# Last block: the first two up-projection tiles on rows without the second row factor, and two feature blocks to an operation

## The reference, cut to what matters

```python
        mix_out = merged @ w_out[l]
        h_res = h_res + rmsnorm_2(mix_out, g_mix_post[l])

        h2 = rmsnorm_2(h_res, g_ffn_pre[l])
        up = centred_dwconv(h2 @ w_up[l], conv_w_ffn[l], conv_b_ffn[l])
        a, v = jnp.split(up, 2, axis=-1)
        ffn_out = (jax.nn.gelu(a) * v) @ w_down[l]
        h_res = h_res + rmsnorm_2(ffn_out, g_ffn_post[l])
```

## Time and profile before

| | |
|---|---|
| median of 3 runs | 1059.67 us (1059.06 to 1060.96) |
| the profiled execution | 1059.63 us |
| its span | 1057.5 us |
| mean granted TensorE clock | 0.986 |
| TensorE matmul busy | 1004.1 us, 95% of the span |
| DVE, ACT, POOL busy | 581.2, 521.3, 521.7 us |
| chain that ended last | PE 71%, DVE 15%, ACT 10%, issue 3%, DMA 1% |

### The profile page before, as it was taken

The page is one execution under the profiler, slowest core; times in us unless marked ns, Lnnn a source line. Parts: engine busy times, 40 slices in busy tenths (PEclk is TensorE's granted clock), DMA queues, the critical chain, the costliest instruction groups (busy, mean ns, idle before and its releaser), DMA issues.

```text
span 1057.5 us, 15122 instructions
## 1 busy us (share of the span) xinstructions
PE 1004.1 (95%) x6334; PEld 897.3 (85%) x6334; DVE 581.2 (55%) x798; ACT 521.3 (49%) x684; POOL 521.7 (49%) x160
## 2 busy tenths in 40 slices
PE   7979999999999998999999999999998799888897
PEld 6867789999888887789998887999898699888775
DVE  4688875888422544546886223262254567777732
ACT  6445446554333566545654334544444554455542
POOL 2433325556666545255566664545444155554572
PEclk9989999999999999999999999999998999999999
DMA  8434314545555443344545555444334243444451
GB/s 318 156 120 159 120 40 162 197 165 194 199 195 183 177 162 128 112 162 160 183 178 198 195 185 200 141 161 170 127 120 159 90 153 139 157 159 160 159 200 40
DMA packets 24787, 168.78 MB, mean 160 GB/s; under 512 B 2784, under 2 KB 3056, under 8 KB 4880
## 3 DMA queue, kind: packets, MB, share of 16 engines
q1 hardware_dynamic: 24432, 167.49, 44.2%
q10 hardware_dynamic: 288, 0.33, 0.1%
HBM read 166.77 MB, written 1.05 MB: 159 GB/s over the span
## 4 chain that ended last, share of the span: by engine, by line
PE 71%; DVE 15%; ACT 10%; issue 3%; DMA 1%; POOL 0%; SPq 0%; DVEq 0%; ACTq 0%
PE bank L607 21%; PE bank L609 21%; PE bank L608 21%; ACT whi L1045 6%; DVE wlo L1570 4%; DVE e L2081 3%; PE bank L795 1%; PE bank L988 1%; ACT e L1524 1%; DVE e L2092 1%; DVE a L1682 1%; PE bank L633 1%; DVE a L1650 1%; ACT e L1531 1%; DMA h<-x_rows 1%
## 5 line engine op out<-in xcount | busy, mean ns | idle before, releaser
L2150 POOL TENSOR_TENSOR wlo<-raw,whi 128x1024 fp32r<-128x1024 f32 (+1 forms) x154 | 520.8, 3385 | 517.1 <-ACT whi L1045 516.9
L1570 DVE TENSOR_TENSOR wlo<-raw,whi 128x1024 fp32r<-128x1024 f32 (+1 forms) x154 | 200.3, 1300 | 350.1 <-ACT whi L1045 350.1
L1045 ACT ACTIVATE whi<-raw 128x2048 fp32r<-128x2048 f32 (+1 forms) x154 | 292.3, 1901 | 143.0 <-PE bank L609 138.6
L607 PE MATMUL bank<-nhi,whi 128*128 128x258 f32 (+3 forms) x1160 | 332.9, 287 | 15.7 <-POOL wlo L2150 11.9
L608 PE MATMUL bank<-nlo,whi 128*128 128x258 f32 (+3 forms) x1160 | 329.0, 284 | 0.0
L609 PE MATMUL bank<-nhi,wlo 128*128 128x258 f32 (+3 forms) x1160 | 327.8, 283 | 0.0
L607 PEld LDWEIGHTS bank<-nhi,whi 128*128 128x128 f32 (+1 forms) x1160 | 220.2, 190 | 23.4 <-issue 22.6
L609 PEld LDWEIGHTS bank<-nhi,wlo 128*128 128x128 f32 (+1 forms) x1160 | 220.8, 190 | 0.0
L608 PEld LDWEIGHTS bank<-nlo,whi 128*128 128x128 f32 (+1 forms) x1160 | 220.6, 190 | 0.1
L607 PE MATMUL bank<-whi,nhi 128*128 128x512 f32 x192 | 80.4, 419 | 6.0 <-POOL wlo L2150 6.0
L608 PE MATMUL bank<-wlo,nhi 128*128 128x512 f32 x192 | 77.7, 405 | 0.0
(11 more groups left out here) (261 smaller groups left out, 1468.5 us busy)
## 6 DMA issues: line engine op xcount, KB each, us to landing
raw<-w_stream SPq DMA_DIRECT2D x154, 1024.0 KB, 4.8
cst<-consts SPq DMA_DIRECT2D x1, 1200.0 KB, 11.5
h<-x_rows SPq DMA_DIRECT2D x4, 256.0 KB, 5.2
raw<-w_stream SPq DMA_DIRECT2D x2, 512.0 KB, 6.5
out_rows<-e SPq DMA_DIRECT2D x4, 256.0 KB, 2.0
b<-consts_x SPq DMA_DIRECT2D x1, 544.0 KB, 5.7
e<-g_post SPq DMA_DIRECT2D x1, 512.0 KB, 3.1
raw<-w_stream SPq DMA_DIRECT2D x1, 352.0 KB, 9.2
```

The costliest lines, as they stand in the source:

```text
L607: pe.matmul(out, lhsT.hi, rhs.hi, start=start, stop=False)
L1045: act.activation(whi[j][:, 0:n], raw[j][:, 0:n], ACT.Copy).then_inc(s_hi.up(i))
L1570: dve.tensor_tensor(wlo[j][:, 0:m], raw[j][:, 0:m], whi[j][:, 0:m].bitcast(F32), ALU.subtract).then_inc(s_lod.up(i))
L2150: pool.tensor_tensor(wlo[j][:, m:n], raw[j][:, m:n], whi[j][:, m:n].bitcast(F32), ALU.subtract).then_inc(s_lop.up(i))
```

## The change

It has five parts.

1. **mo blocks 0 and 1 together.** TensorE first does feature blocks 0 to 5 of both, then 6 and 7 of both. Both `col_add` of their squares stand behind mo block 2.
2. **Two blocks to an operation** of 516 elements in place of two of 258, on DVE (first factor, residual, rest, second factor) and for most of ACT's. `un` and `uhi` count pairs.
3. **Tiles UP2+0 and UP2+1 work on UN**, that is HT by the gain without the second factor (UF), split in two parts as before. The rows of ones and squares (SQ8, eight blocks) are added between the matmuls of UP2+0, two behind each pair of feature blocks; UP2+0 and UP2+2 do `a` and `v` of a feature block in turn.
4. **The factor at the exit.** DVE multiplies the four banks of n = 0 and 1 by RS into SBUF (US). Their taps read US and not the bank. h2 with the factor goes into MG for the tiles from UP2+2 on.
5. **`hi(UP2 + 2)`** and both halves of its `wlo` are moved ahead of the second factor.

```diff
+            us = [begin("mo", g) for g in range(2)]
+            for ks in (range(6), range(6, 8)):
+                for g in range(2):
+                    for k in ks:
+                        on.wait_ge(*s_mglo.at(k))
+                        x = mm3(us[g].t[:, 0:N2], w[:, k, g * P:g * P + P], MG[:, k, :], k == 0, k == 7)
...
-            for k in range(8):
-                col_add(1, k)
             for n in range(22):
...
+                w, x = weights(UP2 + n, 8), UN if n < 2 else MG
+                for av, k in product(range(2), range(8)) if n not in (0, 2) else [(av, k) for k in range(8) for av in range(2)]:
+                    on.wait_ge(*(s_ulo if n < 2 else s_nclo).at(k // 2))
+                    y = mm3(us[av].t[:, 0:N2], w[:, k, av * P:av * P + P], x[:, k, :], k == 0, k == 7)
...
+                    if n == 0 and av == 1 and k % 2:
+                        col_add(1, k - 1)
+                        col_add(1, k)
...
-            for k in range(8):
-                on.wait_ge(*s_ht.at(k))
-                col_square(1, k, HT[:, k, X0:L2])
+            for j in range(4):
+                p = slice(2 * j, 2 * j + 2)
+                on.wait_ge(*s_ht.at(j))
+                for k in (2 * j, 2 * j + 1):
+                    act.activation(UF[:, k, :], HT[:, k, X0:L2], ACT.Copy, scale=vcol("g_ffn_pre", k)).then_inc(s_un.up(j) if k % 2 else own.up())
+                act.activation(UN[:, p, :].hi, UF[:, p, :], ACT.Copy).then_inc(s_uhi.up(j))
+                act.activation(SQ8[:, p, :], HT[:, p, X0:L2], ACT.Square).then_inc(s_sq8.up(j))
+            hi(UP2 + 2)
             col_rms(1)
...
-                on.wait_ge(*s_nc.at(k))
-                act.activation(nT2[:, k, X0:L2].hi, GT[:, k, 0:N2], ACT.Copy).then_inc(s_nhi.up(5, k))
+                on.wait_ge(*s_nc.at(j))
+                act.activation(MG.hi[:, p, :], UF[:, p, :], ACT.Copy).then_inc(s_nchi.up(j))
...
+            for n, av in product(range(2), range(2)):
+                u = use["fu", n, av]
+                on.wait_ge(*u.done())
+                dve.tensor_tensor(US[n][av], u.t[:, 0:N2], RS[:, 0:N2], ALU.mult).then_inc(u.free)
...
-                    dve.scalar_tensor_tensor(out=o, in0=u.t[:, 1:N2 - 1], scalar=vcol("conv_w_ffn", ch), in1=o,
+                    dve.scalar_tensor_tensor(out=o, in0=up[:, 1:N2 - 1], scalar=vcol("conv_w_ffn", ch), in1=o,
```

More of the change, by code:

```diff
@@ L367, in plan_banks @@
             banks.take("fu", n, av)
+        if n == 0:
+            banks.drop("cn", 1)
         last[UP2 + n] = (("fu", n, 1), 0)
@@ L1002, in col_add @@
                 u = begin("cn", c) if k == 0 else use["cn", c]
-                on.wait_ge(*s_sq.at(c, k))
-                pe.matmul(u.t[:, 0:N2], ones, SQ[:, k % 2, 0:N2], start=k == 0, stop=k == 7).then_inc(u.full)
-            for g in range(8):
+                if c == 0:
+                    on.wait_ge(*s_sq.at(k))
+                    x = SQ[:, k % 2, 0:N2]
+                else:
+                    on.wait_ge(*s_sq8.at(k // 2))
+                    x = SQ8[:, k, :]
+                pe.matmul(u.t[:, 0:N2], ones, x, start=k == 0, stop=k == 7).then_inc(u.full)
@@ new lines, in tensor_program @@
+            us = [begin("mo", g) for g in range(2)]
+            w = weights(OUT2, 8)
+            weights_in(OUT2)
+            for ks in (range(6), range(6, 8)):
[3 more added lines that the diff above has]
+                        x = mm3(us[g].t[:, 0:N2], w[:, k, g * P:g * P + P], MG[:, k, :], k == 0, k == 7)
+                    if k == 7:
+                        x.then_inc(us[g].full)
+            for g in range(2, 8):
@@ L1007, in tensor_program, with residual @@
                 feat(weights(OUT2 + g // 2, 8), OUT2 + g // 2, begin("mo", g), g % 2 * P, X0, lambda k: s_mglo.at(k), 8, MG)
[L1008 to L1009 removed]
+                for k in ((0, 1) if g == 2 else (g - 1,)):
+                    col_add(0, k)
             col_add(0, 7)
[L1011 to L1023 removed]
+            def residual(n):
+                tt, c = n // 2, n % 2
+                u = begin("rb", n)
+                for m in range(4):
+                    on.wait_ge(*s_ht.at(c * 2 + m // 2))
+                    x = pe.transpose(u.t[:, m * P:m * P + P], HT[:, c * 4 + m, META + tt * P:META + tt * P + P], ident)
+                x.then_inc(u.full)
@@ L2061, in vector_program, with rows_of @@
             on.wait_ge(*use["resm",].gone())
[L2062 to L2066, removed]
-            on.wait_ge(*s_rs.at(1))
[L2068 to L2075, removed]
+            def rows_of(n):
+                return bc(RS[:, 0:N2].rearrange("p (o t) -> p o t", o=1), [P, n, N2])
@@ new lines, in low_part @@
+            def low_part(dst, j, done):
+                p = slice(2 * j, 2 * j + 2)
+                dve.tensor_tensor(dst[:, p, :].lo, UF[:, p, :], dst[:, p, :].hi.bitcast(F32), ALU.subtract).then_inc(done.up(j))
+            for j in range(5):
+                if j < 4:
+                    p = slice(2 * j, 2 * j + 2)
+                    on.wait_ge(*use["mo", 2 * j].gone())
+                    on.wait_ge(*use["mo", 2 * j + 1].gone())
+                    dve.tensor_tensor(GT[:, 8 + 2 * j:10 + 2 * j, :], GT[:, 8 + 2 * j:10 + 2 * j, :], rows_of(2), ALU.mult).then_inc(own.up())
+                    on.wait_ge(*own.last())
+                    dve.tensor_tensor(HT[:, p, X0:L2], HT[:, p, X0:L2], GT[:, 8 + 2 * j:10 + 2 * j, :], ALU.add).then_inc(s_ht.up(j))
+                if j:
+                    on.wait_ge(*s_uhi.at(j - 1))
+                    low_part(UN, j - 1, s_ulo)
@@ L2077, in ff_mul @@
+            lo(UP2 + 2)
+            on.wait_ge(*s_rs.at(1))
+            for j in range(5):
+                if j < 4:
+                    p = slice(2 * j, 2 * j + 2)
+                    on.wait_ge(*s_ulo.at(j))
+                    dve.tensor_tensor(UF[:, p, :], UF[:, p, :], rows_of(2), ALU.mult).then_inc(s_nc.up(j))
+                if j:
+                    on.wait_ge(*s_nchi.at(j - 1))
+                    low_part(MG, j - 1, s_nclo)
             def ff_mul(n):
```

61 lines of the change are left out of this document (40 added, 21 removed).

## The result

The changed kernel takes **1062.01 us** (median of 20 runs, 1060.58 to 1064.33), the kernel before 1059.67 us (median of 20, 1059.01 to 1061.22). The ratio is 1.0019, with a 95% interval of 1.0012 to 1.0026: slower by some 2 us. That is small, but the interval does not reach 1, so the slowdown is real. It lies on the border that the prediction had set at 0.2%. The profiled execution is one of the faster: 1060.83 us, with a span of 1058.9 us. That is 1.2 us over the profiled execution of before.

The account below looks back on a forecast made before the run. The ring of ACT, POOL and DVE, not TensorE, bounds the kernel: `hi(UP2 + 3)` 1.5 us later plus 0.85 us for the taps of n = 1 makes 2.3 us on 1059.63, so 1061.9 us, range 1059.0 to 1063.9.

Parts of the forecast that it names:

- the border that the prediction had set at 0.2%: The smallest difference from no change that a measurement can tell: 2.1 us, so slower begins at 1061.8 us.
- The ring sets the end: Up-projection: ACT's rounding, POOL's half, ff_mul and Gelu make turns of 6.80 us; their start at `hi(UP2 + 3)` sets the end.
- The first rival: Up-projection: TensorE sets the pace and its lead carries through, giving 1053.8 us; chance 0.11.
- The mo pair: mo blocks 0 and 1: dense TensorE work from block 5 on gains 1.9 us, ends 0.8 and 3.4.
- First matmul of UP2+0: Start of the first up-projection tile: at 830.6 us, 8.6 us earlier than the 839.18 of before.
- UP2+0 with sums and clock: First up-projection tile: 9.3 us for matmuls and eight column sums, plus 1.8 us for 3.6 us at the lower clock.
- the slower rival: UP2+0: the clock stays low for most of the tile, 7 us, giving 1063.6 us; chance 0.16.
- 8.9 us from the sum to `hi(UP2+3)`: Path from the full second column sum to `hi(UP2 + 3)`: 8.9 us where it was 12.64.
- The taps of n = 1: Turn n = 1: taps reading two SBUF operands come behind POOL, costing 0.85 us once, ends 0 and 1.3.
- the rival in which DVE wins: Turn n = 1: the first tap runs ahead of POOL's half, which ends 0.45 us later, giving 1062.4 us; chance 0.08.
- What was costed at nothing: mo blocks 2 to 7, SP's load of the last gains, UP2+2's matmul order and the transposes: no cost.

Follow-up runs that it names:

- e3: The kernel before, with ff_mul(n-1) moved ahead of DVE's half of wlo in each turn: 1040.01 us, ratio 0.9812.
- e1: The kernel before with part 1 of the change alone (mo blocks 0 and 1 together): 1057.12 us, ratio 0.9975.
- e5: The changed kernel with nine matmuls of ones by constants in TensorE's gap ahead of the first pair of UN: 1059.28 us, ratio 1.0003.
- e2: The changed kernel with the exit multiply written back into the bank, which the taps of n = 0 and 1 read: 1061.58 us, ratio 1.0012.
- e6: The changed kernel without seven of the eight column sums of the second factor: 1060.70 us, ratio 1.0003.
- e7: The changed kernel without parts 3 and 4 (no early tiles, no exit multiplies): 1061.29 us, ratio 1.0011.
- e8: As e7, with part 5 undone too (UP2+2 rounded in turn 0 again): 1057.66 us, ratio 0.9977.
- f2: As e4, plus exit factor written back into the bank, nine matmuls in TensorE's gap, and rounding of UP2+3 ahead of turn 0: 1036.27 us, ratio 0.9769.
- e4: The changed kernel with ff_mul(n-1) moved ahead of DVE's half of wlo: 1039.33 us, ratio 0.9802.
- e9: As e8, but UP2+0 and UP2+2 do all of a before v: 1057.92 us, ratio 0.9977.

## Why the prediction was right

The forecast was 1061.9 us, the median is 1062.0. The mechanism was right; that the two agree to 0.1 us is in part luck, as the terms show:

- *The ring sets the end.* Right, and shown by e3. The first rival, that TensorE's lead carries through, is out in this kernel.
- *The mo pair*, 1.9 us (0.8 to 3.4). In e1 2.7 us by the medians. In the profiled execution of the changed kernel the clock did not fall: the first sum came 3.3 us earlier by the mark. The middle was a little low.
- *First matmul of UP2+0*, 8.6 us earlier. It is 10.3 in the trace. Without the 0.75 us upstream, and without the 1.4 us that the mo pair gave beyond the forecast, 8.2 are left.
- *UP2+0 with sums and clock*, 11.1 us. From 828.87 to the last sum near 840.9 it took 12.0. The sums and matmuls came as costed. The clock was low for 5.5 us of it (mean 0.77 over that stretch), between the 3.6 of the forecast and the 7 of the slower rival, so it cost 2.8 us in place of 1.8. e5 shows the term by itself: 2.7 us at the sum.
- *8.9 us from the sum to `hi(UP2+3)`.* 8.88.
- *The taps of n = 1*, 0.85 us. The turn grew by 0.84; shown by e2's trace. POOL's half ran ahead of the tap, which ended 0.27 us behind it: the rival in which DVE wins is out.
- *What was costed at nothing*, but bears on the variants: POOL's half of UP2+2. I named its end (841.2) and its cover, the late factor, but not what it costs once the cover goes. e5 (0.6 us), e6 (1.3 us) and e7 (2.1 us on DVE; 3.6 us in the times of e7 and e8) paid it. In the changed kernel as it stands it ends at 839.97, ahead of the factor.

So terms were off against each other in the profiled execution: the mo pair gave 1.4 us more than forecast, while the way to the first tile and the clock in it took 1.2 us more. `hi(UP2+3)` comes 1.3 us later by the mark, where 1.5 was forecast, and the rest of the span is 2.2 us longer, where 2.3 was. The whole profiled execution is only 1.2 us over that of before, mainly since it came 0.75 us earlier to the mark. The clock at the mo blocks, low before and not in the changed kernel, is a chance of these executions: e2 and e6, with the same order there, had it low. That the 20 runs average this out is my reading; their clocks in this stage are not on record.

What I had wrong was an account that came after the prediction: for e7 I put the loss on the early tiles alone. Without them and with the moved rounding (e7) the time is the same; without both (e8) the loss is gone. So the moved rounding alone holds the ring back, by POOL's half and the longer wait of TensorE that follows. With the early tiles there, TensorE's pace does it (e5, e6). Whether the early tiles alone, without the moved rounding, cost as much stays open: that was not run. And in f2 it is not told apart which of its three additions to e4 brought the 3.1 us.

## What to carry to other kernels

Where an engine with 95% busy time waits a little for the same releaser in each turn of equal turns, look for a ring of the others, and for what in it is in line behind an operation that it does not need; a lead on the bound-looking engine is worth nothing until that is moved, and moving one instruction was worth seven times the other single edit of the kernel before (19.8 us against the 2.7 of e1). Work that is put into a waiting engine's gap is free only while the gap is there: sums and early matmuls took the second factor's own path. And when a rounding is moved, follow POOL's half of it to its end, since the DVE operations with two SBUF inputs that come then stand behind it (e7: 3.44 us in place of 1.30).

## What the hardware showed that I had not expected

- Kernels that are alike up to the mo blocks differ in the clock there: over 800 to 805 us the mean was 0.70 in e9 and 1.00 in e8, behind the same idle gap of 2.01 us. From the mark, the first sum came 1.5 us later in e9. The single runs of one kernel spread by as much or more; that the clock is the cause there is argued and not shown.
- Behind 4.97 us of idleness from 823.9 us on, the clock was low for 6.9 us in all, worked out from the means of the three stretches (0.76, 0.55 and 1.00). Nine matmuls of ones in that gap, 4.08 us together, kept it at 1.00 (e5).
- POOL's half of a tile takes 2.40 us where it starts first (f2), and 3.4 us where DVE's half of 1.23 us does.
